# The order of the 24 products of a weight piece between the two PSUM banks of its tiles

## Chip, cores and metric

One NeuronCore of one Trainium2 chip runs the whole program. The metric is the device time of one execution in microseconds (us), lower is better; a time is given as the median of several runs. One further execution is recorded by the hardware profiler, and all rows of a trace below come from that one.

## What is computed

One layer of a decoder trunk is applied to 256 prompt tokens and 8 sample tokens, 264 columns in all, in fp32. Nearly all the arithmetic is in products of the normalised activations with large weight matrices:

```python
D_MODEL = 2048; SEQ = 256; DEC_BATCH = 8; D_FF = 5632; PLE_DIM = 256
xn = rmsnorm(h, attn_norm)
proj = xn @ w_in                       # q, k, v, z, a, b, sB, sC, sh, gA, gB
...                                    # short convolutions, gated delta rule in chunks
y_a = o @ w_gdn_out
y_b = (sB * conv) @ w_sconv_out
h = h + (sigmoid(gA) * y_a + sigmoid(gB) * y_b) @ w_o
hn = rmsnorm(h, ffn_norm)
h = h + (silu(hn @ w_ffn_gate) * (hn @ w_ffn_up)) @ w_ffn_down
hn = rmsnorm(h, ple_norm)
h = h + sigmoid(hn @ w_ple_gate) * (p @ w_ple_proj)
y = rmsnorm(h, final_norm)             # and the new states of the delta rule and of both convolutions
```

## The kernel before

The program is written engine by engine; the order of each engine's work is the order of the code, and semaphores join them. The weights stream through once. They are cut into **pieces**: 512 rows of a matrix (four contraction tiles of 128) by 256 columns, 512 KB. There are 828 pieces, in phases (`first`, `group1` to `group7`, `last_group`, `sb`, `gates`, `yb`, `ya`, `wo`, `ffn`, `down`, `pproj`, `pgate`). The phases `down` and `pproj` have some pieces of three or two contraction tiles.

A piece goes through four engines. SyncE issues the transfer into one of four slots of `raw`. ScalarE (L1004) copies it, rounded to fp32r, into a slot of `whi`; VectorE (L1329) puts the remainder `raw - whi` into the same slot of `wlo` and raises `lo_ready`. Both work three pieces ahead. The activations are split in the same way into `xhi` and `xlo` (`ahi`, `alo` for the second product of the FFN, `phi`, `plo` for the embedding). TensorE then makes for each contraction tile k three products, whi x xhi, whi x xlo and wlo x xhi, in fp32r, and adds them up in PSUM; the fourth, of both remainders, is left out.

The 256 columns of a piece are two **tiles** of 128 output rows, t = 0 and 1, and each tile has a PSUM bank of its own. A **pair** is the set of pieces (four in most phases) that add up to the same two tiles. Pairs alternate between banks 0 and 1 and banks 2 and 3 (`par`), so that VectorE and ScalarE can read out one pair's banks while TensorE fills the other's. Banks 4 to 7 serve the small matmuls of the delta rule, the transposes and the sums, which stand between pieces (`extra`).

TensorE's loop over pieces is `body`. Before a pair it waits for `pair_free` of its banks, before a piece for `xlo_ready` (or `a_ready`) and `lo_ready`. The last product of a piece raises `piece_used`. On it hang ScalarE's next write into the weight slot (L1004, four pieces on) and, for the last piece of a pair, the reading of both banks by VectorE (`evac`) and by ScalarE. One pair, of kind `ab`, has a single tile. Each call of `mm` is a weight load and a matmul; with plain fp32 operands, as in the delta rule, the hardware's records have two of each for one call.

Of the kernel before, what the change touches and what calls it, by code (L numbers as in the profile page):

```python
# [37 lines left out]
P = 128  # L38
# [43 lines left out]
def trunk(nc, I, O):  # L82
# [3 lines left out]
    N = T + NB  # L86
# [34 lines left out]
    def new(name, shape, dt=F32):  # L121
        t = at(name, shape, dt, top[0])
        top[0] += size(shape, dt)
        return t

    raw = new("raw", [P, RAW, KT, COLS])
    whi = new("whi", [P, SPLIT, KT, COLS], F32R)
    wlo = new("wlo", [P, SPLIT, KT, COLS], F32R)
# [99 lines left out]
    with ctx:  # L228
        bank = [ctx.enter_context(nc.psum_tensor(f"bank{i}", [P, 512], F32)) for i in range(8)]
# [175 lines left out]
        def piece(ph, it, j):  # L405

            return it * ph.pieces + (ph.p0 + j + 1)
# [289 lines left out]
        def _(pe):  # L697
            pe.sem_inc(sct_turned, 1)

            def mm(out, lhsT, rhs, start=True, stop=True):  # L700
                return pe.matmul(out, lhsT, rhs, start=start, stop=stop)  # L701
# [229 lines left out]
            def body(ph, it):  # L931
                j = 0
                for qi, q in enumerate(ph.pairs):
                    n = ph.q0 + qi
                    par = n % 2
                    if n >= 2:
                        pe.wait_ge(pair_free[par], it * (len(ph.pairs) // 2) + n // 2)
                    kt, last = 0, sum(q.kts) - 1
                    for m_ in q.kts:
                        if q.rhs[0] is ahi:  # L940
                            pe.wait_ge(a_ready, FP * int(q.xready[3:]) + (kt + m_ + 1) // 2)
                        else:
                            pe.wait_ge(xlo_ready, XR[q.xready] + kt + m_)
                        pe.wait_ge(lo_ready, piece(ph, it, j))
                        sl = (ph.p0 + j) % SPLIT
                        for t in range(q.tiles):
                            for k in range(m_):
                                out = bank[2 * par + t][:, 0:N]
                                w = (whi[:, sl, k, t * P:(t + 1) * P], wlo[:, sl, k, t * P:(t + 1) * P])
                                mm(out, w[0], q.rhs[0][:, kt + k, :], kt + k == 0, False)  # L950
                                mm(out, w[0], q.rhs[1][:, kt + k, :], False, False)
                                m = mm(out, w[1], q.rhs[0][:, kt + k, :], False, kt + k == last)
                        m.then_inc(piece_used, 1)
                        kt += m_
                        extra(ph, it, j)
                        j += 1

            def work(when, ph, it):
                if when == "body":
                    return body(ph, it)  # L960
                if ph.name == "first":
                    pe.wait_ge(ident_ready, 1)
                    for _ in range(12):
                        mm(bank[7][:, 0:P], ident[:, :], ident[:, :])
                    pe.wait_ge(x_in[0], 16 * (BLK + 2))
                    pe.transpose(bank[7][:, 0:DTL], arow[:, :], ident[0:DTL, 0:DTL]).then_inc(vec_turned, 1)
                    for kt in range(DTL):
                        if kt % 4 == 0 and kt > 0:
                            pe.wait_ge(x_in[kt // 4], 16 * (BLK + 1))
                        if kt == 7:  # L970
                            pe.wait_ge(vec_ready, 1)
                        if kt >= 8:
                            pe.wait_ge(h_copied if kt % 2 == 0 else h_copied_odd, (kt - 8) // 2 + 1)
                        for b in range(BLK):
                            pe.transpose(bank[kt % 8][:, b * P:(b + 1) * P], xrow[:, b, kt * P:(kt + 1) * P], ident[:, :])
                        pe.transpose(bank[kt % 8][:, T:N], xrow[0:NB, BLK, kt * P:(kt + 1) * P], ident[0:NB, 0:NB]).then_inc(x_turned, 1)
                    pe.wait_ge(h_copied, 5)
                    pe.wait_ge(h_copied_odd, 5)
# [841 lines left out]
```

## Time and profile before

| | us |
|---|---|
| median of 3 runs | 2594.24 |
| lowest and highest of the 3 | 2591.71, 2597.14 |
| profiled execution, its own time | 2590.02 |
| span of the profiled execution, first to last instruction | 2588.2 |

The mean granted clock of TensorE over the span is 0.994 of full speed. A profile shows when each instruction started and for how long it was under way. Matmuls overlap in the pipeline, so that the mean duration of one is longer than its share of the time; the distance from one start to the next is what counts. PE is TensorE's matmul, PEld its weight load, DVE VectorE, ACT ScalarE, POOL GpSimd, SP SyncE.

### The profile page before, as it was taken

Reading aid. Unit: us, or ns where it says so; the run is one execution under the profiler, and the core shown is the slowest. Engines: PE = TensorE matmul, PEld = TensorE weight load, DVE = VectorE, ACT = ScalarE, POOL = GpSimd, SP = SyncE. Lnnn points to the kernel's source line nnn. Section 1 sums busy time; section 2 is a strip of 40 time slices with the busy share of each in tenths; the row PEclk is TensorE's granted clock in tenths of the full one; section 3 lists DMA queues with packets and bytes.
Section 4 is the critical chain, followed back from the end, with each engine's and each line's share of the span. In section 5 each row is a group of like instructions: output and inputs, shape, how many; then the busy total and the mean of one; then the engine's idle time right before and its main releaser. Section 6 shows DMA issues by size and latency. Waiting matters only on the chain.

```text
span 2588.2 us, 50479 instructions
## 1 busy us (share of the span) xinstructions
PE 2541.3 (98%) x20848; PEld 2519.6 (97%) x20848; DVE 1664.2 (64%) x2861; ACT 1321.2 (51%) x2013; POOL 512.9 (20%) x913
## 2 busy tenths in 40 slices
PE   7999999999999999999999999999999999999997
PEld 6999999999999999999999999999999999999997
DVE  6767768586777765533365566566776656776665
ACT  6555646464554644333344344445665546565663
POOL 1526254352716340000000000100110000110100
PEclk8999999999999999999999999999999999999999
DMA  7656565555646556677755566758986767985563
GB/s 216 184 156 177 145 176 150 164 170 147 195 138 176 146 163 196 181 211 211 204 165 181 182 201 196 244 180 255 313 280 215 220 189 253 315 281 186 164 207 108
DMA packets 445718, 507.38 MB, mean 196 GB/s; under 512 B 21329, under 2 KB 423914, under 8 KB 443066
## 3 DMA queue, kind: packets, MB, share of 16 engines
q1 hardware_dynamic: 417072, 415.43, 53.0%
q0 software_dynamic: 27840, 88.53, 11.2%
q8 instruction: 166, 2.72, 0.4%
q14 instruction: 62, 0.51, 0.1%
q10 hardware_dynamic: 578, 0.19, 0.0%
HBM read 478.16 MB, written 26.49 MB: 195 GB/s over the span
## 4 chain that ended last, share of the span: by engine, by line
PE 92%; DVE 3%; ACT 2%; DMA 1%; issue 1%; DVEq 0%; POOL 0%; ACTq 0%; POOLq 0%
PE bank L701 91%; DVE wlo L1329 1%; ACT whi L1004 1%; DMA raw<-in_w_ffn_down 1%; DVE E L1408 1%; DVE vTok L1475 0%; PE bank L781 0%; DMA raw<-in_w_ple_gate 0%; PE bank L770 0%; DVE cacc L1503 0%; ACT sqr L1237 0%; PE bank L725 0%; DVE xlo L1369 0%; ACT xhi L1297 0%; ACT vTok L1103 0%
## 5 line engine op out<-in xcount | busy, mean ns | idle before, releaser
L701 PE MATMUL bank<-xhi,whi 128*128 128x264 f32 x5520 | 1591.5, 288 | 7.7 <-DVE wlo L1329 4.7
L701 PE MATMUL bank<-xlo,whi 128*128 128x264 f32 x5520 | 1568.6, 284 | 0.0
L701 PE MATMUL bank<-xhi,wlo 128*128 128x264 f32 x5520 | 1566.3, 284 | 0.0
L1329 DVE TENSOR_TENSOR wlo<-raw,whi 128x1024 fp32r<-128x1024 f32 x828 | 1012.9, 1231 | 728.4 <-ACT whi L1004 727.7
L1004 ACT ACTIVATE whi<-raw 128x1024 fp32r<-128x1024 f32 x828 | 871.9, 1058 | 809.5 <-PE bank L701 735.0
L701 PEld LDWEIGHTS bank<-xhi,whi 128*128 128x128 f32 x5520 | 1041.3, 189 | 10.8 <-issue 7.2
L701 PEld LDWEIGHTS bank<-xlo,whi 128*128 128x128 f32 x5520 | 1042.0, 189 | 2.0 <-issue 1.9
L701 PEld LDWEIGHTS bank<-xhi,wlo 128*128 128x128 f32 x5520 | 1038.9, 188 | 0.0
L701 PE MATMUL bank<-ahi,whi 128*128 128x264 f32 x704 | 200.2, 284 | 1.9 <-DVE wlo L1329 1.9
L701 PE MATMUL bank<-ahi,wlo 128*128 128x264 f32 x704 | 200.2, 284 | 0.0
L701 PE MATMUL bank<-alo,whi 128*128 128x264 f32 x704 | 199.7, 284 | 0.0
L553 POOL TENSOR_TENSOR sol<-sol,prod 128x60 f32<-128x60 f32 (+24 forms) x248 | 132.3, 534 | 19.4
L701 PEld LDWEIGHTS bank<-ahi,whi 128*128 128x128 f32 x704 | 132.4, 188 | 2.3 <-issue 2.2
L701 PEld LDWEIGHTS bank<-ahi,wlo 128*128 128x128 f32 x704 | 132.6, 188 | 0.0
L701 PEld LDWEIGHTS bank<-alo,whi 128*128 128x128 f32 x704 | 132.3, 188 | 0.0
L550 POOL TENSOR_TENSOR prod<-blk,sol 128x60 f32<-128x60 f32 (+24 forms) x248 | 106.8, 431 | 48.7 <-issue 14.1
L1503 DVE SCALAR_TENSOR_TENSOR cacc<-cin,vec,cacc 128x288 f32<-128x288 f32 x224 | 108.6, 526 | 4.0
L659 POOL DMA_DIRECT2D out_gdn_s<-sS x16 | 18.7, 1171 | 427.0 <-DVE sS L1753 427.0
L567 POOL DMA_DIRECT2D blk_scratch<-Tt x32 | 19.0, 602 | 345.9 <-DVE Tt L1439 343.9
L1259 ACT ACTIVATE sS<-sS,bc 128x128 f32<-128x128 f32 x256 | 81.2, 391 | 0.0
L1753 DVE SCALAR_TENSOR_TENSOR sS<-sD,kqs,sS 128x128 f32<-128x128 f32 x256 | 72.5, 345 | 0.0
L630 POOL DMA_DIRECT2D chunkS<-in_state_gdn x16 | 18.5, 1155 | 260.9 <-PE bank L701 227.4
(300 smaller groups left out, 1822.1 us busy)
## 6 DMA issues: line engine op xcount, KB each, us to landing
raw<-in_w_in SPq DMA_DIRECT2D x356, 512.0 KB, 4.1
raw<-in_w_ffn_gate SPq DMA_DIRECT2D x88, 512.0 KB, 5.4
raw<-in_w_ffn_up SPq DMA_DIRECT2D x88, 512.0 KB, 4.8
raw<-in_w_ffn_down SPq DMA_DIRECT2D x96, 384.0 KB, 3.5
raw<-in_w_gdn_out SPq DMA_DIRECT2D x64, 512.0 KB, 3.5
chunkS<-in_state_gdn POOLq DMA_DIRECT2D x16, 1024.0 KB, 7.4
raw<-in_w_sconv_out SPq DMA_DIRECT2D x32, 512.0 KB, 3.4
raw<-in_w_o SPq DMA_DIRECT2D x32, 512.0 KB, 4.0
```

The source lines that it names most:

```text
L550: mine.inc(pool.tensor_tensor(prod[:, 0:m, 0:n], blk[:, j, j + 1:SB].unsqueeze(1).to_broadcast([P, m, n]), sol[:, 0:m, j:j + 1].to_broadca ...
L553: mine.inc(pool.tensor_tensor(sol[:, 0:m, j + 1:SB], sol[:, 0:m, j + 1:SB], prod[:, 0:m, 0:n], ALU.add))
L567: pool.dma_start(blk_d[:, b, :, :].rearrange("m j i -> j m i"), Tt[SB * b:SB * b + SB, :, :].rearrange("p c (i t) -> p (c i) t", i=4)[:, : ...
L630: pool.dma_start(chunkS[:, c, :, :], I["state_gdn"][0, b, 16 * c:16 * c + 16, :, :].rearrange("h k v -> k h v")).then_inc(s_in[c], 16)
L659: pool.dma_start(O["gdn_s"][0, 2 * b2 + s, 16 * c:16 * c + 16, :, :].rearrange("h k v -> k h v"), sS[:, s, :, :]).then_inc(n_stored[s], 16)
L701: return pe.matmul(out, lhsT, rhs, start=start, stop=stop)
L1004: act.activation(whi[:, at_ % SPLIT, :, :], raw[:, at_ % RAW, :, :], ACT.Copy).then_inc(hi_ready, 1)
L1259: m = act.activation(sS[:, s, i, :], sS[:, s, i, :], ACT.Copy, scale=bc[:, ds(it * 2 + (s + 1), 1), 16 * c + i:16 * c + i + 1].rearrange(" ...
L1329: dve.tensor_tensor(wlo[:, at_ % SPLIT, :, :], raw[:, at_ % RAW, :, :], f32(whi[:, at_ % SPLIT, :, :]), ALU.subtract).then_inc(lo_ready, 1)
L1408: m = dve.scalar_tensor_tensor(out=E[:, c, s], in0=Gv[:, i, c, :], scalar=col(tok, 0, c, hd(i)), in1=later[:, :], op0=ALU.subtract, op1=AL ...
L1503: m = dve.scalar_tensor_tensor(out=cacc[:, t, :], in0=x, scalar=w, in1=cacc[:, t, :], op0=ALU.mult, op1=ALU.add)
L1753: m = dve.scalar_tensor_tensor(out=sS[:, s, i, :], in0=sD[:, s, i, :], scalar=kqs[:, 8 * c + i // 2, ds(it * 2 + s, 1), 0], in1=sS[:, s, i ...
```

## The change

In `body` the loops over the tiles and over the contraction tiles change places. Before, all products of tile 0 came first, 12 in a row into its bank, then the 12 of tile 1. Now, for each contraction tile, each of the three products is made for tile 0 and directly afterwards for tile 1. The order of the three parts changes too: whi x xhi, wlo x xhi, whi x xlo. The flag that starts a sum stands on the first product into each bank, the flag that ends it on the last into each.

```diff
-                        for t in range(q.tiles):
-                            for k in range(m_):
-                                out = bank[2 * par + t][:, 0:N]
-                                w = (whi[:, sl, k, t * P:(t + 1) * P], wlo[:, sl, k, t * P:(t + 1) * P])
-                                mm(out, w[0], q.rhs[0][:, kt + k, :], kt + k == 0, False)
-                                mm(out, w[0], q.rhs[1][:, kt + k, :], False, False)
-                                m = mm(out, w[1], q.rhs[0][:, kt + k, :], False, kt + k == last)
+                        for k in range(m_):
+                            for part, (w, x) in enumerate(((whi, q.rhs[0]), (wlo, q.rhs[0]), (whi, q.rhs[1]))):
+                                for t in range(q.tiles):
+                                    m = mm(bank[2 * par + t][:, 0:N], w[:, sl, k, t * P:(t + 1) * P], x[:, kt + k, :],
+                                           kt + k == 0 and part == 0, kt + k == last and part == 2)
                         m.then_inc(piece_used, 1)
```

TensorE, before, the middle of a piece of the phase `first`, from the last contraction tile of tile 0 to the first of tile 1. `bank0<-xhi_52,whi_50` reads: into bank 0, moving operand `xhi`, weights `whi`.

```order
L701 MATMUL bank0<-xhi_52,whi_50 128x264
L701 MATMUL bank0<-xlo_53,whi_50 128x264
L701 MATMUL bank0<-xhi_52,wlo_51 128x264
L701 MATMUL bank1<-xhi_52,whi_50 128x264
L701 MATMUL bank1<-xlo_53,whi_50 128x264
L701 MATMUL bank1<-xhi_52,wlo_51 128x264
```

The same six places of the stream after the change:

```order
L701 MATMUL bank1<-xhi_52,wlo_51 128x264
L701 MATMUL bank0<-xlo_53,whi_50 128x264
L701 MATMUL bank1<-xlo_53,whi_50 128x264
L701 MATMUL bank0<-xhi_52,whi_50 128x264
L701 MATMUL bank1<-xhi_52,whi_50 128x264
L701 MATMUL bank0<-xhi_52,wlo_51 128x264
```

The bank changed once in these six rows and now changes at each; the weights of two neighbouring products are never the same block now (the two `whi` rows are the two tiles' halves), and the moving operand is the same in twos.

TensorE, before, in the phase `gates`: the end of a piece, the small products with the states (`chunkS`) between two pieces, and the beginning of the next.

```order
L701 MATMUL bank3<-xhi_52,whi_50 128x264
L701 MATMUL bank3<-xlo_53,whi_50 128x264
L701 MATMUL bank3<-xhi_52,wlo_51 128x264
L701 MATMUL bank4<-kqs_109,chunkS_108 128x2 x4
L701 MATMUL bank2<-xhi_52,whi_50 128x264
L701 MATMUL bank2<-xlo_53,whi_50 128x264
L701 MATMUL bank2<-xhi_52,wlo_51 128x264
```

After:

```order
L701 MATMUL bank3<-xhi_52,wlo_51 128x264
L701 MATMUL bank2<-xlo_53,whi_50 128x264
L701 MATMUL bank3<-xlo_53,whi_50 128x264
L701 MATMUL bank4<-kqs_109,chunkS_108 128x2 x4
L701 MATMUL bank2<-xhi_52,whi_50 128x264
L701 MATMUL bank3<-xhi_52,whi_50 128x264
L701 MATMUL bank2<-xhi_52,wlo_51 128x264
```

The small products stand at the same place between the pieces, and the number of rows is the same. Nothing moves on the other engines.

## Rows read from the trace of the kernel before

**Rows 1.** The page: span, and busy time (share of span) and instructions of each engine.
```profile
span 2588.2 us, 50479 instructions
PE 2541.3 (98%) x20848; PEld 2519.6 (97%) x20848; DVE 1664.2 (64%) x2861; ACT 1321.2 (51%) x2013; POOL 512.9 (20%) x913
```

**Rows 2.** The page: the chain that ended last, shares by engine, then by line.
```profile
PE 92%; DVE 3%; ACT 2%; DMA 1%; issue 1%; DVEq 0%; POOL 0%; ACTq 0%; POOLq 0%
PE bank L701 91%; DVE wlo L1329 1%; ACT whi L1004 1%; DMA raw<-in_w_ffn_down 1%; DVE E L1408 1%; DVE vTok L1475 0%; PE bank L781 0%; DMA raw<-in_w_ple_gate 0%; PE bank L770 0%; DVE cacc L1503 0%; ACT sqr L1237 0%; PE bank L725 0%; DVE xlo L1369 0%; ACT xhi L1297 0%; ACT vTok L1103 0%
```

**Rows 3.** Waits: who waited for whom: us in total, times, longest us.
```profile
ACT whi L1004 <- PE bank L701: 735.0, 494, 2.8
...
PE bank L701 <- DVE wlo L1329: 6.6, 5, 2.3
```

**Rows 4.** The page's groups: line, engine, operation, count | busy us, mean ns | idle before.
```profile
L701 PE MATMUL bank<-xhi,whi 128*128 128x264 f32 x5520 | 1591.5, 288 | 7.7 <-DVE wlo L1329 4.7
L701 PE MATMUL bank<-xlo,whi 128*128 128x264 f32 x5520 | 1568.6, 284 | 0.0
L701 PE MATMUL bank<-xhi,wlo 128*128 128x264 f32 x5520 | 1566.3, 284 | 0.0
L1329 DVE TENSOR_TENSOR wlo<-raw,whi 128x1024 fp32r<-128x1024 f32 x828 | 1012.9, 1231 | 728.4 <-ACT whi L1004 727.7
L1004 ACT ACTIVATE whi<-raw 128x1024 fp32r<-128x1024 f32 x828 | 871.9, 1058 | 809.5 <-PE bank L701 735.0
L701 PEld LDWEIGHTS bank<-xhi,whi 128*128 128x128 f32 x5520 | 1041.3, 189 | 10.8 <-issue 7.2
L701 PEld LDWEIGHTS bank<-xlo,whi 128*128 128x128 f32 x5520 | 1042.0, 189 | 2.0 <-issue 1.9
L701 PE MATMUL bank<-ahi,whi 128*128 128x264 f32 x704 | 200.2, 284 | 1.9 <-DVE wlo L1329 1.9
```

**Rows 5.** Busy time by stretch: engines' busy us (instructions), TensorE clock, DMA share, GB/s.
```profile
core 0: us, PE busy (x) PEld busy (x) DVE busy (x) ACT busy (x) POOL busy (x), PEclk, DMA share, GB/s
1360.00:1900.00 540.00, 540.00 (x4458) 539.87 (x4457) 336.94 (x508) 261.63 (x396) 34.65 (x33) 1.00 0.71 223
2460.00:2463.00 3.00, 3.00 (x16) 3.00 (x15) 1.39 (x2) 2.62 (x5) 1.64 (x2) 0.50 0.49 131
```

**Rows 6.** Timeline of TensorE, two pieces: start us, duration us, instruction.
```profile
1436.69 0.28 PE L701 MATMUL bank<-xhi,whi 128*128 128x264 f32 x1
...
1438.01 0.28 PE L701 MATMUL bank<-xhi,wlo 128*128 128x264 f32 x1
1438.13 0.28 PE L701 MATMUL bank<-xhi,whi 128*128 128x264 f32 x1
...
1439.46 0.28 PE L701 MATMUL bank<-xhi,wlo 128*128 128x264 f32 x1
1439.58 0.28 PE L701 MATMUL bank<-xhi,whi 128*128 128x264 f32 x1
...
1442.50 0.28 PE L701 MATMUL bank<-xhi,whi 128*128 128x264 f32 x1
```

**Rows 7.** Timeline of TensorE in a delta-rule step that alternates between two banks.
```profile
497.54 0.38 PE L701 MATMUL bank<-Tt,Nn 128*128 128x128 f32 x2
...
498.65 0.28 PE L701 MATMUL bank<-QK,Tt 128*128 128x128 f32 x1
```

**Rows 8.** Timeline of TensorE around 2460 us, where its clock is lower.
```profile
2458.88 0.39 PE L701 MATMUL bank<-phi,whi 128*128 128x264 f32 x1 [3.70 <-DVE h L1656]
...
2459.85 0.42 PE L701 MATMUL bank<-plo,whi 128*128 128x264 f32 x1
2460.07 0.42 PE L701 MATMUL bank<-phi,wlo 128*128 128x264 f32 x1
...
2462.93 0.42 PE L701 MATMUL bank<-phi,whi 128*128 128x264 f32 x1
2463.15 0.32 PE L701 MATMUL bank<-plo,whi 128*128 128x264 f32 x1
```

## Prediction

> **What bounds the kernel now.** I read the page's table of busy times first. TensorE is busy for 2541.3 of 2588.2 us; VectorE for 1664.2 and ScalarE for 1321.2 [rows 1]. A busy matmul row proves little by itself, since the rows overlap, so the second view is the chain that ended last: 92% of it is TensorE, and 91% the single line through which all matmuls go [rows 2]. Third, the waits: TensorE waited 6.6 us in all, in 5 waits, for the split of the weights, while ScalarE waited 735.0 us for TensorE to hand back a weight buffer [rows 3]. So the weights are always ready, and the pace of the matmuls sets the end. Fourth, the groups of instructions: the products are 3 groups of 5520 and 3 of 704 (one of these stands for all three), which is 18,672, all 128x264, and each has its own weight load (5520 loads beside each 5520 matmuls; two of the three stand) [rows 4]. The mean durations there, 284 to 288 ns, are those of overlapping rows and are not the price of a product. The price is the spacing: between 1360 and 1900 us TensorE ran 4458 matmuls in 540.00 us at a granted clock of 1.00 with no gap, so **121.1 ns each** [rows 5]. 18,672 x 0.1211 = 2261 us of the 2588.2 us go to products. What remains, 327 us, is the small matmuls of the delta rule, transposes, start and end, which the change doesn't touch.
>
> **What the change does to TensorE's stream.** Count and shape of products stay: 24 in a whole piece, each with its weight load. What changes is what stands next to what. (a) Before, a piece has two switches of bank, one in its middle and one where the next piece begins; afterwards every product switches, 22 more in each piece of 24. (b) Before, in 8 of 24 transitions the same weight block is loaded twice in a row; afterwards never. (c) Before, the moving operand changed at nearly every product (xhi, xlo, xhi); afterwards it stands twice in a row and changes at every second product.
>
> **The price of a bank switch (a)** can be read off, for the kernel already does it. In the piece that starts at 1436.69, the 12th product starts at 1438.01 and the 13th, in the other bank, at 1438.13: 0.12 us. The 24th starts at 1439.46 and the first of the next piece at 1439.58: 0.12 again [rows 6]. These rows round to 10 ns. Over the 687 whole pieces of the trace the start times, which are kept to 1 ns, give a mean of 121.1 ns from 12th to 13th and 121.3 ns between neighbours in one bank (first and last rows of such a piece stand in the group). For transitions from piece to piece that mean is 120.2 ns in the calm stretch after 1400 us, and 121.9 before 900 us. So the bounds of a switch are -1 and +0.6 ns, and the middle is zero. Two other places say the same. In the delta rule's step that alternates between banks 5 and 6, two passes (a matmul of full fp32 is run as two) take 0.22 us: from 497.54 to 498.65 it is ten passes, 111 ns each [rows 7], while two passes of one product, which add into one bank back to back, have the same spacing. And where the clock was granted at only 0.50 (that is 1.2 GHz), products follow each other from 2460.07 to 2462.93 in 13 steps, 220 ns each [rows 5, 8]: exactly 264 columns at 1.2 GHz. There six products go into one bank, then six into the other; nothing is lost to adding into the same bank, and nothing at the switch. I take 0 ns x 22: **0 us**, with bounds of -1 x 22/24 x 18,672 = -17 us and +0.6 x 22/24 x 18,672 = +10 us.
>
> **The weight loads (b).** The trace shows a load for every matmul, the repeated ones (xlo, whi) too, with the same 189 ns as the others [rows 4]. A repeat is thus not skipped today and there is nothing to lose. 0 us.
>
> **New neighbours (c).** At full clock 264 columns would stream in 110 ns, and the short matmuls above are spaced at 111 ns, so about 10 ns a product go to something else. It isn't the bank, by the rows above; it is also not fixed. Within a piece the spacing swings between 116 and 130 ns, in a pattern that repeats to 1 ns with every second piece. The even piece takes 2.89 us for 24 products (1436.69 to 1439.58), which is 120.4 ns each; the odd piece that follows takes 2.92 us (to 1442.50), 121.7 ns each [rows 6]. Same number, same shapes, same order; only the buffers that are read beside one another differ, or where the clocks stand. A new order of reads makes a new pattern. No row tells which. Its mean could lie anywhere that present patterns lie: 18,672 x (120.4 - 121.1) = -13 us, 18,672 x (121.7 - 121.1) = +11 us. I take the present mean, since it averages over many pairings of buffers: **0 us**.
>
> **Other engines.** A tile's sum for the first bank is complete later than before (at the end of the pair's last piece, not in its middle), but VectorE and ScalarE begin their reading of both banks when the last piece is used up, as before. The release of the weight buffer hangs on the piece's last product in both orders. Nobody's wait moves. The one pair with a single tile (the decays' columns, 4 pieces) only has its three parts in another order. SyncE's and GpSimd's streams are as before.
>
> **Against the Trainium skill.** 18,672 products at 121.1 ns is what the rows show [rows 5]. The Trainium skill, in "TensorE: Matmul & The Clock Gate", section "Back-to-back issue gap", lets the spacing depend on the columns and on the weight load, N/2.4 + 2.5 ns for a matmul alone, 112.5 ns here; the bank is no term of it. By that page the change would be worth 0 us too, but its figure is 8.6 ns under this trace, 161 us over all products, and it has no name for those.
>
> **Sum.** 0 + 0 + 0 on the profiled run's 2590.02 us (span 2588.2). That run lies 4 us under the median of 2594.24; the three runs reach from 2591.71 to 2597.14. I forecast the median: 2594.
>
> **Rivals.**
> 1. *Adding into the same bank does cost* and alternation hides it. All of the 10 ns can't go, since loading weights sets a floor near 111 to 112 ns [rows 7]; at most 18,672 x (121.1 - 112) = 170 us, so 2424 us; a small part, 1 ns, gives 2594 - 17 = 2577. Against it: the switch in the middle of a piece brings no shorter spacing, and at half clock adding in place costs nothing. For it: only that 10 ns are unexplained, and the lowest mean for a switch between pieces, 120.2 ns. If products did get faster, ScalarE's 1058 ns and VectorE's 1231 ns a piece have room under 2.9 us [rows 4].
> 2. *A better pattern of neighbours*, by (c): down to 2594 - 13 = 2581 us.
> 3. *A worse pattern of neighbours*, the one that ends slower: the same mechanism, where the pace of today's odd piece or worse becomes that of all: 2594 + 11 = 2605 us. It decides from a mean spacing of 121.4 ns up (0.3 ns x 18,672 = 5.6 us). For it: the piece with this pace is in the trace, with identical work. Nothing hides it, for TensorE has 47 us of idle time in all [rows 1].
> 4. *The clock drops.* In the trace the granted clock falls to 0.50 after TensorE stood idle for 3.70 us before 2458.88, for want of its banks, and products then cost 220 ns in place of 121 [rows 5, 8]. The 15 products from 2459.85 to 2463.15 cost 15 x 99 ns = 1.5 us more than at full clock. Should alternation make TensorE pause and drop like this once in every second piece, that is 414 x 1.5 = 620 us, a time of about 3210 us. Against it: there is no gap at today's switches. The Trainium skill, same page, section "A second HAM failure mode: psum-queue depth-cycling", tells of a kernel that cycled through banks, paused shortly between groups, and whose clock swung; by that rule this change would hurt.
>
> **Chances.** About 0.2% (5 us) is what a measurement of this kernel can tell from no change. Same, 2589 to 2599: 0.48. Faster: rival 1 large 0.05, rival 1 small or rival 2 0.24, together 0.29. Slower: rival 3 0.21, rival 4 0.02, together 0.23. The likeliest case's own range is 2589 to 2599. The range that I give reaches to the ends of rivals 2 and 3 and a little past them, for the bounds of (a) and (c) may add in part: 2579 to 2607. It leaves out rival 1 large, rival 4, and the tails of the others, less than 2 in 10.
>
> **What would show it.** In the trace afterwards: 1360 to 1900 us again holds 4458 matmuls within 11 if the forecast is right; 4470 or more speak for rivals 1 and 2, 4446 or fewer for rival 3. Rival 1 shows as *every* spacing shorter, with a lowest value below 116 ns; rivals 2 and 3 as a new pattern of unlike spacings that repeats with every second piece. Under rival 4 the granted clock is below 1.00 in the long stretches. The waits must stay as small as in [rows 3]. I am wrong if the spacing's mean moves by over 0.3 ns; then a price that I set at zero had one, and the step at fault is (a) if the pattern is even, (c) if it isn't.

## The result and the profile after

| | before | after |
|---|---|---|
| median, us | 2592.97 (4 runs) | 2609.74 (4 runs) |
| lowest and highest | 2590.59, 2597.14 | 2608.52, 2613.15 |
| span of the profiled execution | 2588.2 | 2611.4 |

The ratio is 1.0061, with a 95% interval of 1.0047 to 1.0076: the change costs 0.6%, 17 us. The profiled execution of after is the longest of its four.

The page of after: its span and busy times, and the chain that ended last by engine. These answer to [rows 1, 2].

```profile
span 2611.4 us, 50479 instructions
...
PE 2561.5 (98%) x20848; PEld 2539.6 (97%) x20848; DVE 1664.0 (64%) x2861; ACT 1321.2 (51%) x2013; POOL 512.2 (20%) x913
...
PE 90%; DVE 3%; ACT 2%; DMA 2%; POOL 1%; issue 1%; DVEq 0%; POOLq 0%; ACTq 0%
```

TensorE is busy for 20 us more, no other engine is. Its share of the chain is 90%, after 92%; no other engine's rises by more than a point. The waits of after, beside [rows 3] (who waited for whom, us in total, times, longest):

```profile
ACT whi L1002 <- PE bank L701: 752.3, 504, 2.8
...
PE bank L701 <- DVE wlo L1327: 7.2, 4, 2.2
```

TensorE still waits for nobody, 7.2 us against 6.6; ScalarE waits 17 us longer for TensorE. So no new wait has come in: the products themselves are slower. The stretch from 1360 to 1900 us, to be held against [rows 5] (busy us and instructions of PE, PEld, DVE, ACT, POOL, then clock, DMA share, GB/s):

```profile
core 0: us, PE busy (x) PEld busy (x) DVE busy (x) ACT busy (x) POOL busy (x), PEclk, DMA share, GB/s
1360.00:1900.00 540.00, 540.00 (x4408) 539.87 (x4407) 329.37 (x492) 255.65 (x380) 32.35 (x30) 1.00 0.69 217
```

4408 matmuls where 4458 stood, at the same clock of 1.00 and with no gap: 122.5 ns a product, 1.4 more than before. On TensorE's timeline (start us, duration us, instruction; x2 are two products one behind the other) an even and an odd piece begin at

```profile
1449.06 0.40 PE L701 MATMUL bank<-xhi,whi 128*128 128x264 f32 x2
...
1451.99 0.41 PE L701 MATMUL bank<-xhi,whi 128*128 128x264 f32 x2
...
1454.94 0.40 PE L701 MATMUL bank<-xhi,whi 128*128 128x264 f32 x2
```

2.93 and 2.95 us, where [rows 6] have 2.89 and 2.92. The slowdown isn't even. These are the 48 spacings of an even and an odd piece in ns, averaged over some 40 such couples between 1425 and 1670 us, worked out from the start times of the trace; within the stretch each agrees to about 0.5 ns from one couple to the next:

```
before (mean 121.1)
even: 123 117 122 119 120 123 124 117 121 121 116 121 123 119 120 121 123 119 123 121 121 118 120 118
odd:  118 120 120 124 122 122 118 120 123 129 120 121 121 126 122 121 127 122 119 121 121 121 122 122
after (mean 122.5)
even: 118 121 122 120 116 122 125 123 121 120 124 119 123 122 121 119 121 121 124 122 127 126 127 127
odd:  121 126 123 124 127 122 123 121 119 126 122 122 118 120 122 127 130 132 123 122 122 118 118 122
```

It is a new pattern, between 116 and 132 ns, that again repeats with every second piece; the shortest spacing is as short as it was.

### The profile page after: what moved, and what is told of

It reads as the page before. It is cut to its first block, busy times and chain, and to the rows that moved or that the text cites. A ratio compares the mean times of both kernels' runs of the same rounds, so it can differ in the third digit from the quotient of the medians.

```text
span 2611.4 us, 50479 instructions
## 1 busy us (share of the span) xinstructions
PE 2561.5 (98%) x20848; PEld 2539.6 (97%) x20848; DVE 1664.0 (64%) x2861; ACT 1321.2 (51%) x2013; POOL 512.2 (20%) x913
## 4 chain that ended last, share of the span: by engine, by line
PE 90%; DVE 3%; ACT 2%; DMA 2%; POOL 1%; issue 1%; DVEq 0%; POOLq 0%; ACTq 0%
PE bank L701 89%; DMA raw<-in_w_ffn_down 1%; DVE wlo L1327 1%; ACT whi L1002 1%; POOL prod L550 1%; DVE E L1406 1%; POOL sol L553 1%; DVE vTok L1473 0%; DMA raw<-in_w_ple_gate 0%; DMA blk<-blk_scratch 0%; PE bank L781 0%; PE bank L770 0%; ACT sqr L1235 0%; PE bank L725 0%; DMA DT<-sol_scratch 0%
## 5 line engine op out<-in xcount | busy, mean ns | idle before, releaser
L701 PE MATMUL bank<-xhi,whi 128*128 128x264 f32 x5520 | 1147.6, 289 | 7.3 <-DVE wlo L1327 4.3
L701 PE MATMUL bank<-xlo,whi 128*128 128x264 f32 x5520 | 1127.6, 286 | 0.0
L701 PE MATMUL bank<-xhi,wlo 128*128 128x264 f32 x5520 | 1123.9, 284 | 0.0
L701 PEld LDWEIGHTS bank<-xhi,whi 128*128 128x128 f32 x5520 | 860.4, 189 | 12.3 <-issue 8.5
L701 PEld LDWEIGHTS bank<-xlo,whi 128*128 128x128 f32 x5520 | 859.7, 189 | 0.0
L701 PEld LDWEIGHTS bank<-xhi,wlo 128*128 128x128 f32 x5520 | 857.9, 189 | 0.0
L701 PE MATMUL bank<-ahi,whi 128*128 128x264 f32 x704 | 143.0, 284 | 2.9 <-DVE wlo L1327 2.9
L701 PE MATMUL bank<-alo,whi 128*128 128x264 f32 x704 | 143.2, 284 | 0.0
L701 PE MATMUL bank<-ahi,wlo 128*128 128x264 f32 x704 | 142.5, 284 | 0.0
L701 PEld LDWEIGHTS bank<-ahi,wlo 128*128 128x128 f32 x704 | 108.9, 188 | 0.0
```

## Experiments: banks or reads

The change alters two things at once: the bank that each product goes into, and the order in which operands are read. The first two runs part them. Each run has a short name (e1, e2 and so on), and above its result stands in a quote what was expected of it. Of `body`, the banks alone (e1):

```diff
+i_ = 0
 for t in range(q.tiles):
     for k in range(m_):
         for w, x in ((whi, q.rhs[0]), (whi, q.rhs[1]), (wlo, q.rhs[0])):
-            m = mm(bank[2 * par + t][:, 0:N], ...)
+            m = mm(bank[2 * par + i_ % q.tiles][:, 0:N], ...)
+            i_ += 1
```

> The reads stay exactly as before (12 products of tile 0, then 12 of tile 1, whi xhi, whi xlo, wlo xhi); only the bank that a product is added into alternates at every product, so the two banks hold mixed sums and the output is not the layer's. If a switch of bank costs (step (a) of the prediction, mis-priced), the whole loss of the change is here: about 2610 us, some 4408 matmuls between 1360 and 1900 us and a spacing of 122.4 ns. If the order of the reads costs (step (c)), this runs as before: 2593 us, 4458 matmuls, 121.1 ns, and the same pattern of spacings as before (120.4 ns in the even piece, 121.7 in the odd one).

And the reads alone (e2), the loops as in the changed kernel and `bank[2 * par + i_ // (3 * m_)]` for the bank:

> The mirror of the first: weights and moving operands are read exactly in the changed kernel's order, but the first 12 products of a piece go into one bank and the last 12 into the other, so the sums are mixed and the output is not the layer's. If the switch of bank costs: as before, 2593 us and 121.1 ns. If the order of the reads costs: as the changed kernel, 2610 us and 122.4 ns, with the last three spacings of an even piece at 126 to 127 ns as there.

The stretch of e1, then that of e2:

```profile
1360.00:1900.00 540.00, 540.00 (x4458) 539.87 (x4457) 337.06 (x510) 261.14 (x392) 33.49 (x31) 1.00 0.70 223
```

```profile
1360.00:1900.00 540.00, 540.00 (x4407) 539.87 (x4406) 330.52 (x496) 257.48 (x387) 32.31 (x30) 1.00 0.69 218
```

e1 took 2594.08 us, 1.0005 of before (0.9995 to 1.0014), with before's 4458 matmuls; its pattern is before's to within 1 ns in each of its spacings. e2 took 2607.83 us, 1.0059 (1.0044 to 1.0074), with 4407, and its pattern is after's, each spacing to within 1 ns. Twenty-two more switches of bank a piece cost nothing and save nothing that these runs can tell. The loss is in the order of the reads.

## Experiments: which of the reads

The next two take the order of the parts and the interleaving of the tiles one at a time.

```diff
 # e3: tiles outside as before
-        for w, x in ((whi, q.rhs[0]), (whi, q.rhs[1]), (wlo, q.rhs[0])):
+        for w, x in ((whi, q.rhs[0]), (wlo, q.rhs[0]), (whi, q.rhs[1])):
 # e4: tiles inside as in the changed kernel
-        for w, x in ((whi, q.rhs[0]), (wlo, q.rhs[0]), (whi, q.rhs[1])):
+        for w, x in ((whi, q.rhs[0]), (whi, q.rhs[1]), (wlo, q.rhs[0])):
```

> Tiles stay outside, 12 products in a row into a bank; only the order of the three parts is the changed kernel's (whi xhi, wlo xhi, whi xlo). The moving operand then stands twice in a row and the weights never. If a repeated weight block was worth something before, or the part order is at fault: 2600 to 2610 us. If it is the interleaving of the tiles: 2593 us. If every new order draws a pattern of its own: a third pattern, anywhere from 2580 to 2610 us.

> The tiles alternate at every product as in the changed kernel, with the parts in the old order (whi xhi, whi xlo, wlo xhi). If the interleaving (of banks or of weight halves) is at fault: 2610 us. If the part order is: 2593 us. If every order draws its own pattern: a fourth pattern, anywhere from 2580 to 2610 us.

e3: 2594.59 us, 1.0005 (0.9995 to 1.0014). e4: 2606.99 us, 1.0056 (1.0041 to 1.0071). The interleaving is at fault. What surprised me was that neither has a pattern of its own: e3's spacings are before's, e4's are after's. Whether whi or wlo, xhi or xlo is read leaves no mark in this layout, where a row of xlo starts at the same place within 256 bytes as the row of xhi with its number (xhi is 16 x 1056 = 66 x 256 bytes long). In e3 two neighbouring products never read the same weight block, as in the changed kernel, and xhi stands for two products; neither costs anything.

Two things remain that the interleaving reorders: the halves of the weight blocks, and the rows of the activations. Before, the row number k stays for three products and the four rows are gone through twice; afterwards it stays for six, once. e5 and e6 cross the two orders (the code is e5's; in e6 `order_w` and `order_x` are exchanged):

```diff
+order_w = [(t, k, p_) for k in range(m_) for p_ in range(3) for t in range(q.tiles)]   # new
+order_x = [(t, k, p_) for t in range(q.tiles) for k in range(m_) for p_ in range(3)]   # old
+for i_, ((t, k, p_), (_, kx, px)) in enumerate(zip(order_w, order_x)):
+    w, x = (whi, whi, wlo)[p_], (q.rhs[0], q.rhs[1], q.rhs[0])[px]
+    m = mm(bank[2 * par + i_ // (3 * m_)][:, 0:N], w[:, sl, k, t * P:(t + 1) * P], x[:, kt + kx, :], ...)
```

> The weight blocks are read in an order with the tiles inside (the two halves of whi, the two halves again, the two halves of wlo, then the next contraction tile), the moving rows in the order of the kernel before (a row for three products, the four rows twice in a piece), 12 products into each bank. Weights and rows that don't belong together are multiplied, so the output is not the layer's. Theory WEIGHTS (the jump between the halves of a weight block is what costs): as the changed kernel, about 2608 us, 122.4 ns in the stretch 1360 to 1900 us. Theory ROWS (what matters is how long the moving operand stays at one row: three products before, six now): as before, 2593 us and 121.1 ns. If only the pairing of a weight address with a row address matters: a pattern of its own.

> The mirror: weights as before (12 of one half, 12 of the other), moving rows in the new order (each row for six products, once in a piece); not the layer's output either. Theory WEIGHTS: 2593 us, 121.1 ns. Theory ROWS: 2608 us, 122.4 ns, with the last spacings of an even piece at 127 ns. Pairing: a pattern of its own.

The same stretch, of e5 and of e6:

```profile
1360.00:1900.00 540.00, 540.00 (x4458) 539.87 (x4457) 337.10 (x508) 261.52 (x395) 33.50 (x31) 1.00 0.70 223
```

```profile
1360.00:1900.00 540.00, 540.00 (x4407) 539.87 (x4406) 331.06 (x496) 257.57 (x387) 32.30 (x30) 1.00 0.69 217
```

e5: 2594.77 us, 0.9999 (0.9989 to 1.0008), before's pattern. e6: 2608.78 us, 1.0056 (1.0041 to 1.0071), after's pattern. So which weight block is read plays no part either; the sequence of the moving operand's rows makes the spacings. One thing these runs can't tell: every block of whi and wlo starts at the same place within 512 bytes (slots are 4096 bytes apart, contraction tiles 1024, halves 512), so a weight block with another start was never read.

## Experiments: what about the rows

The rows of xhi are 264 x 4 = 1056 bytes apart, which is 32 beyond a multiple of 256; a piece's four rows are 4224 bytes, 128 beyond. The pattern repeats after two pieces. That suggested the start of a row within 256 bytes. e7 moves all rows by 128.

```diff
+    top[0] += 128
     xhi = new("xhi", [P, DTL, N], F32R)
```

> The kernel before with 128 bytes of empty memory ahead of xhi, so that xhi, xlo and all that lie behind them move by 128 bytes, whi and wlo not; a right result. The rows of the moving operand are 1056 bytes apart, four rows 4224, which is 128 beyond a multiple of 256, and the pattern of spacings repeats with every second piece. If the moving operand's address within 256 bytes makes the pattern: the patterns of even and odd pieces trade places (even 121.75 ns, odd 120.55), at the same total of 2593 us. If the slot of the weights (even or odd) or anything else that counts pieces makes it: nothing changes (even 120.55).

The starts of an even piece, an odd one and the next even one in e7:

```profile
1438.75 0.28 PE L702 MATMUL bank<-xhi,whi 128*128 128x264 f32 x1
...
1441.67 0.28 PE L702 MATMUL bank<-xhi,whi 128*128 128x264 f32 x1
...
1444.57 0.28 PE L702 MATMUL bank<-xhi,whi 128*128 128x264 f32 x1
```

2.92 us for the even and 2.90 for the odd piece, in place of 2.89 and 2.92. The two patterns have traded places: turned by 24 products, before's 48 spacings differ from e7's by 0.13 ns on average, unturned by 3.0. The total stays, 2593.03 us, 0.9998 (0.9988 to 1.0009). A move by 128 bytes changes the pattern, and a step of two pieces, which are 256 bytes apart modulo 512, doesn't: among the powers of two, the modulus is 256. I take xhi to begin at a start of 128; then the even pieces of before read rows with starts 128 to 224, the odd ones 0 to 96. No trace keeps addresses, so this origin isn't shown. The argument uses only distances: with another origin, all starts named here and below shift alike. The weights stayed where they were; whether the start as such counts, or its distance from that of the weights, these runs leave open.

e8 takes the change from row to row away.

> The order of the kernel before, but all products of a piece read the piece's first row of the activations (not the layer's output). If the change from row to row or the rows' alignment costs: a flatter pattern in the piece, with spacings that differ less than today's 116 to 130 ns, and a mean that shows the price of rows whose start is a multiple of 256 or of 128 bytes; if near the 112 ns of the short matmuls, alignment is the whole excess. If rows play no part: the pattern and 121.1 ns as before.

The edit is `x[:, kt, :]` for `x[:, kt + k, :]`. It took 2600.71 us, 1.0024 (1.0014 to 1.0034), and my guess of a flat pattern was wrong in a telling way. Here are the spacings inside three odd pieces, all with the same start 0 for all 24 products, and inside two even ones with start 128:

```
odd,  start 0:    123 122 124 127 123 122 124 123 124 122 125 122 124 123 124 122 125 122 124 123 124 122 125
odd,  start 0:    121 124 121 119 120 120 120 120 120 120 120 120 120 120 120 120 120 120 120 120 120 120 120
odd,  start 0:    119 119 121 126 122 124 127 123 122 124 123 124 122 125 122 124 123 124 122 125 122 124 123
even, start 128:  125 116 120 121 125 125 115 120 121 126 124 116 120 121 126 124 116 120 121 125 125 115 120
even, start 128:  125 126 120 123 120 120 120 120 120 120 120 120 120 120 120 120 120 120 120 120 120 120 120
```

With one row for all products, the spacing settles into a cycle, and into which one differs from piece to piece: a steady 120 ns, or a swing about 123, or five steps from 115 to 126 (116, 120, 121, 126, 124). The reads repeat with every second piece, the slots of the weights with every fourth; but the spacings repeat with every sixth. Even pieces go steady, five steps, five steps, and the odd pieces behind them swing, swing, steady, over and over from 1400 to 1675 us, to within 1 ns, and again after an interruption by small matmuls. The pairs and the weight slots have a period of four pieces and the banks one of eight; none has six. So a spacing is not the price of a start; something is carried over from product to product and from piece to piece, and the sequence of starts drives it. e11 repeats this with other starts.

> As e8 (all products of a piece read the piece's first row, not the layer's output), with xhi and all behind it moved by 32 bytes: the rows read start at 160 and 32 within 256 bytes, in place of 128 and 0. If the start makes the price: two other means than e8's 121.2 ns (start 128) and 122.2 ns (start 0), each steady through a piece; the start with the lowest price shows how rows should lie.

> As the one before with 64 bytes: starts 192 and 64. If the price depends on the start within 128 bytes, both pieces cost the same here, and differ from e8's two.

One run each: 2605.92 us and 2590.97 us. With a move of 32 bytes the even pieces cycle through 118, 124, 125 ns and the odd through 122, 122, 121; with 64 bytes all odd pieces fall into the steady 120 after some products of up to 131. In the stretch 1360 to 1900 us they have 4431 and 4452 matmuls. The second expectation, the same cost for both kinds of piece, failed in its pattern and held roughly in its means (121.2 and 121.3 ns inside the pieces); that these would differ from both of e8's failed too, for e8 has 121.2 ns in its even pieces.

## Experiments: is interleaving dear as such?

If a longer stay at one row were what costs, a stay of one product should be cheapest. e9 has one:

```diff
-    for k in range(m_):
-        for w, x in ((whi, q.rhs[0]), (whi, q.rhs[1]), (wlo, q.rhs[0])):
+    for w, x in ((whi, q.rhs[0]), (whi, q.rhs[1]), (wlo, q.rhs[0])):
+        for k in range(m_):
```

> Tiles outside, then the three parts, then the contraction tiles: the moving row changes at every product (rows 0 to 3 of xhi, 0 to 3 of xlo, 0 to 3 of xhi), a row never stands for two products. A right result. If the stay at one row costs by its length (one, three and six products): below the kernel before, 2580 to 2590 us, under 121.0 ns in the stretch 1360 to 1900 us. If each order of rows only draws a pattern of its own without such a rule: anywhere from 2585 to 2610 us.

2591.12 us, 0.9993 (0.9984 to 1.0002), and 4468 matmuls in the stretch, 120.9 ns. The spacing is under the 121.0 ns that the rule asked for, the time is not in its range of 2580 to 2590 us, and by the bound of 0.2% it is no change. The rule fails with e8, where 24 products on a row are cheaper (121.7 ns) than six. e9's pattern is short: 121, 121, 117, 122 over and over in the even pieces (120.1 ns), 119, 119, 122, 126 in the odd ones (121.3). e10 goes back to the old order and moves xlo alone.

> The order of the kernel before, with 128 bytes of empty memory between xhi and xlo, so that a row of xlo no longer starts at the same address within 256 bytes as the row of xhi. A right result. Theory: only the sequence of starts within 256 bytes makes the pattern. Then a new pattern appears, where e7 kept the old one with its pieces exchanged; its mean may be either side of 121.1 ns, within 120.4 to 122.9. If the pattern stays as before, the address of the row isn't what matters.

The edit is a `top[0] += 128` ahead of `xlo`. 2592.73 us, 0.9999 (0.9990 to 1.0008), with a pattern of its own and 121.4 ns: a move of xlo alone changes the pattern, a move of both together kept it.

The decisive pair, g1 and g2, keeps the changed kernel's loops and moves the rows.

> The changed kernel with 32 bytes of empty memory ahead of xhi; a right result. Its moving rows follow each other in memory, six products each, so their starts within 256 bytes run through the same circle of eight values all the time, and a move by 32 bytes only turns this circle by one row against the pieces. If the sequence of starts is all that matters: the same pattern earlier or later by six products, the same mean of 122.4 ns, 2608 us. If the place of a start within the piece matters: another mean.

> The changed kernel with 128 bytes between xhi and xlo; a right result. Interleaving, six products on a row number, and banks are as in the changed kernel, but two of the six now start 128 bytes further within 256. If interleaving costs as such: 122.4 ns and 2608 us again. If only the sequence of starts costs: another pattern with another mean, most likely nearer to the 121.2 ns of all other patterns seen, 2590 to 2600 us.

g1 took 2606.95 us, 1.0053 (1.0040 to 1.0067). Its pattern is after's, turned by exactly six products: mean difference 0.4 ns turned, 3.5 unturned. The place in the piece doesn't matter, the sequence does. g2 took 2596.36 us, 1.0013 (1.0004 to 1.0022). The stretch in g1, then in g2:

```profile
1360.00:1900.00 540.00, 540.00 (x4407) 539.87 (x4406) 333.15 (x500) 257.82 (x388) 32.32 (x30) 1.00 0.68 218
```

```profile
1360.00:1900.00 540.00, 540.00 (x4443) 539.87 (x4442) 336.02 (x507) 260.38 (x391) 33.53 (x31) 1.00 0.69 222
```

With the very interleaving of the changed kernel, 128 empty bytes take 13 of its 17 us away. The 4 us that are left are of the size of the moves that layout makes in the old order too, as the next run, g3, shows.

> The kernel before with 64 bytes ahead of xhi; a right result. Here a piece goes through its four rows twice, so a move by two rows isn't a rotation but another sequence (starts 192, 224, 0, 32 twice, then 64 to 160 twice). Sequence theory: a new pattern, mean anywhere from 120.4 to 122.4 ns, 2580 to 2608 us. If the old order is good as such: 121.1 ns and 2593 us.

2598.50 us, 1.0022 (1.0012 to 1.0031), 121.5 ns. The old order isn't good as such: 64 bytes make it 0.2% slower. Nor is e9's, as g5 shows:

> The order of e9 (another row at every product) with 64 bytes ahead of xhi; a right result. e9's pieces with starts 128 to 224 cost 120.1 ns a product, those with 0 to 96 121.3 ns. Here each piece's four starts are 192 to 32 or 64 to 160. If the dear spacings belong to certain steps between starts: a mean between 120.1 and 121.3 ns in other shares, 2575 to 2595 us; at 120.1 ns in both pieces it would be 2574 us and beat both kernels.

2601.31 us, 1.0032 (1.0019 to 1.0044), 121.8 ns. My range of 120.1 to 121.3 ns was a miss: I had treated the spacings as prices of steps that could be shared out anew, and they aren't.

## A version that is faster than both

e9's even pieces hold the cheapest steady pattern that I had seen. Instead of guessing the sum of a new sequence, h1 gives its odd pieces, and the xhi products of all, the very same starts; h2 puts the order of the kernel before on this layout.

```diff
-    xhi = new("xhi", [P, DTL, N], F32R)
+    xhi_t = new("xhi", [P, DTL // KT, KT * N + 32], F32R)   # 128 bytes behind every four rows
+    top[0] -= 128                                           # the last gap isn't needed
     xlo = new("xlo", [P, DTL, N], F32R)
...
+    class Rows:
+        def __getitem__(self, ix):
+            p_, kt_, c_ = ix
+            g_, r_ = kt_ // KT, kt_ % KT
+            return xhi_t[:, g_, r_ * N:(r_ + 1) * N]
```

> The order of e9 (another row at each product), with 128 bytes of empty memory behind every four rows of xhi, so that its rows start at 128, 160, 192 and 224 within 256 bytes in every piece; xlo stays dense, its rows start at 0 to 96 in the even pieces and at 128 to 224 in the odd ones. A right result. Sequence theory: the odd pieces now read the very sequence of e9's even pieces, pattern 121, 121, 117, 122 and 120.1 ns; the even ones a new one, 120.1 to 121.5 ns. Together about 120.1 to 120.8 ns in the long stretch, 2575 to 2590 us, which would beat both kernels. If the start of a row isn't all that counts: 120.8 ns and 2591 us as e9.

> The same layout with the order of the kernel before (a right result). Sequence theory: the odd pieces read the starts that the even pieces of the kernel before read; after a piece of another kind the pattern may begin differently. About 120.5 to 121.5 ns, 2582 to 2600 us.

h1 took 2583.04 us (2580.31 to 2585.56, 5 runs), **0.9959 of before, 0.9946 to 0.9971**, the only version clear of before on the faster side by more than 0.2%, and 27 us under the changed kernel. The span and the stretch:

```profile
span 2581.2 us, 50479 instructions
...
PE 2531.0 (98%) x20848; PEld 2508.8 (97%) x20848; DVE 1661.8 (64%) x2861; ACT 1321.9 (51%) x2013; POOL 514.4 (20%) x913
```

```profile
1360.00:1900.00 540.00, 540.00 (x4488) 539.87 (x4488) 340.13 (x517) 265.74 (x406) 35.24 (x33) 1.00 0.71 225
```

4488 matmuls, 120.3 ns. The pattern:

```
even: 117 122 121 121 116 119 122 126 121 120 122 121 117 122 121 121 116 119 122 126 121 120 122 121
odd:  117 122 121 121 117 122 121 121 117 122 121 121 117 122 121 121 117 122 121 121 117 122 121 121
```

The odd pieces repeat e9's even ones but for the first two spacings, as the theory had it. h2, the same layout with before's order, took 2590.89 us, 0.9989 (0.9980 to 0.9998), with before's mean of 121.1 ns and other spacings. Its odd pieces read the starts that before's even pieces read, and yet agree with them to within 1 ns without a break only over the last seven spacings (1.8 ns of difference on average over the 24). The starts within a piece alone don't fix its spacings; what went before it lasts for most of a piece.

Orders and layouts in one view, by the mean of the 48 spacings in the calm stretch (ns) and the ratio to before:

| kernel | order of rows | layout | ns | ratio |
|---|---|---|---|---|
| before | 3 products a row | dense | 121.1 | 1 |
| after | 6 | dense | 122.5 | 1.0061 |
| e7 | 3 | all + 128 | 121.1 | 0.9998 |
| g1 | 6 | all + 32 | 122.5 | 1.0053 |
| g2 | 6 | xlo + 128 | 121.5 | 1.0013 |
| g3 | 3 | all + 64 | 121.5 | 1.0022 |
| e10 | 3 | xlo + 128 | 121.4 | 0.9999 |
| e9 | 1 | dense | 120.8 | 0.9993 |
| g5 | 1 | all + 64 | 121.8 | 1.0032 |
| h1 | 1 | xhi groups at 128 | 120.3 | 0.9959 |
| h2 | 3 | xhi groups at 128 | 121.1 | 0.9989 |

## Why the prediction was wrong

- *What bounds the kernel*: right. TensorE waits for nobody before and after, and each tenth of a ns in the spacing reaches the end. The change in the spacing is 1.4 ns between 1400 and 1900 us, 0.8 ns after that, and less among the delta rule's steps before 1000 us (0.66 and 0.38 ns inside even and odd pieces). Over all products this adds up to about 16 us, beside 17 us between the medians and 23 us between the two profiled spans.
- *(a) the bank switch at 0 ns, bounds -17 and +10 us*: the value is right. e1 measures 1 us for 22 switches a piece, and its interval of the ratio takes in 1. The bounds were misread. The 120.2 ns between pieces belongs to rows, not to banks. The 121.9 ns before 900 us isn't a price at all: 112 transitions there follow each other directly, with a mean of 120.0 ns, and only with the seven of 147 to 153 ns that have a small matmul in between does the mean come near 122.
- *(b) the repeated weight load at 0*: right, by e3 and e5.
- *(c) new neighbours, 0 us, bounds -13 and +11 us*: **this step failed.** Its mechanism was named and is the true one, a new order of reads makes a new pattern. Two things in it were wrong. It looked for the pattern in the pairing of buffers, but which weight block stands beside a row has no part in it (e5, e6). And its bounds took the even and the odd piece of the present pattern (120.4 and 121.7 ns) for the ends of what any pattern may be. The measured 122.5 ns lies outside: +1.4 ns x 18,672 = 26 us at the calm stretch's rate, where 11 stood. Even the 17 us that were measured over the whole program are 0.9 ns a product, past the bound of 0.6. The lower end isn't one either, for h1 has 120.3 ns. The range ended at 2607 and the time is 2609.74.
- *What stands twice*: in the changed order xhi stands for four products in a row and xlo for two, not each for two, as the account of the change and step (c) have it. It alters no sum, since e4, with xhi, xhi, xlo, xlo, xhi, xhi, has after's spacings.
- *Taking the present mean as the middle*, because it averages over many pairings: half right. The eleven rows of the table have means from 120.3 to 122.5 ns; before's 121.1 is indeed near their middle. But their spread of about 0.7 ns around it is 13 us, far more than the 5 us that I gave to "same" with a chance of 0.48. With what the trace already showed, a 14 ns swing within a piece, same deserved less.
- *Rival 1* (adding into one bank costs) is refuted by e1: alternation alone leaves every spacing as it was, to within 1 ns. *Rival 2* exists as a possibility, as h1 shows, but the changed kernel doesn't have it. *Rival 3* came true: the pattern is uneven and slower, as its sign said (4408 matmuls, under 4446). *Rival 4* didn't happen: the granted clock is 1.00 in the stretch, as before, and the Trainium skill's case of a clock that swings when banks are cycled ("TensorE: Matmul & The Clock Gate", section "A second HAM failure mode: psum-queue depth-cycling") isn't met here: with a switch at every product TensorE was busy for all 540.00 us of the stretch.
- The figure that the Trainium skill gives on the same page, section "Back-to-back issue gap", for a matmul alone, 112.5 ns with 264 columns, was and is under every mean here (120.3 to 122.5), and it has no term for what moved the time.

**What stays open** is the mechanism under the rows. The runs show that the start of the moving row within 256 bytes drives it, that it keeps a state from product to product, and that neither the bank nor the choice of the weight block enters; a weight block with another start within 256 bytes was not tried. At half clock it is absent: 220 ns in all 13 steps [rows 8], in `pproj`, with the rows of phi. Rows of xhi and xlo show the same. At the start of the kernel before, where the granted clock is 0.50 (16 to 22 us), the first spacing is 358 ns and the next 17 are 219 to 221 ns; then, as the clock rises, come 124, 118 and 119 ns. Which part of the path between SBUF and the array holds the state was not tried, and no model of mine gives the 48 spacings from the starts.

## What to carry to other kernels

When TensorE is the bound at full clock and the mean spacing is above what the columns alone need, list the spacings between starts over some repeats of the loop: here a pattern that repeats to 1 ns was the sign that the order and the layout of the moving operand have a price. A change of loop order can then have a cost that its purpose doesn't tell, from -0.4 to +0.6% here; try it with two or three layouts (some empty bytes ahead of a tile) before its idea is judged. And an experiment that swaps one aspect of the order while it freezes the others, even with meaningless sums, settles in one run what the trace of before can only bound.

## What the runs showed of the hardware that I had not expected

- The spacing of fp32r products of 264 columns at a granted clock of 1.00 is 115 to 132 ns, and repeats to about 0.5 ns over the more than 80 pieces between 1425 and 1670 us. A move of the moving tiles by 128 bytes exchanges the patterns of even and odd pieces.
- 24 products on one row can run at a steady 120 ns, in five steps from 115 to 126 ns or at a swing about 123 ns; which of them comes repeats with every sixth piece, while the reads repeat with every second (e8).
- A switch of bank at each product, and the read of another weight block at each, leave every single spacing where it was, to within 1 ns (e1, e3, e5), with all weight blocks at the same start within 512 bytes.
- 128 bytes of empty memory changed the time of a 2.6 ms kernel by 0.5% (between the changed kernel at 2609.74 us and g2 at 2596.36), with no instruction added.
